# Norm roots as powers on GpSimd, silu as tanh, in a streaming-encoder layer on one core

## The reference, cut to what matters

```python
def rms_scale(x):
    return x * lax.rsqrt(jnp.mean(x * x, axis=-1, keepdims=True) + 1e-6)

h = rmsnorm(x, g_mix)                       # norm 1
q, k, v, g, gb, gc, hc = split(h @ w_in)    # 4 x 512 and 3 x 512 columns
o = rms_scale(retention(rotary(q), rotary(k), v))   # norm 2, for each of 4 heads
o = o * jax.nn.silu(g)
c = gb * short_conv(gc * hc)
x = x + concat([o, c]) @ w_out
h = rmsnorm(x, g_ffn)                       # norm 3
# peer(h), for each row: 8 heads x 16 chosen experts of 16384
act = gelu(dot(h, u_tab[eidx]));  x = x + sum(gate * act * v_tab[eidx])
y = rmsnorm(x, g_final)                     # norm 4
```

## Time and profile before

| | |
|---|---|
| median of 3 runs | 3035.3 us (3033.67 to 3039.89) |
| the profiled execution, its own time | 3035.47 us |
| span from its first to its last instruction | 3033.6 us |
| TensorE, VectorE, ScalarE, GpSimd busy | 76%, 68%, 67%, 40% of the span |
| moved by DMA | 1226.64 MB, mean 404 GB/s; the gathers 1107.36 MB of it |
| mean granted TensorE clock | 0.846 |

### The profile page before, as it was taken

How to read it: one execution, slowest core, us unless ns; L and a number is a source line. 1 busy time by engine, 2 the same in 40 slices (tenths; PEclk the granted TensorE clock), 3 DMA queues, 4 the chain that set the end, 5 groups by cost and what they waited for, 6 DMA issues and landing times.

```text
span 3033.6 us, 36636 instructions
## 1 busy us (share of the span) xinstructions
PE 2303.3 (76%) x12800; PEld 1880.0 (62%) x12800; DVE 2067.1 (68%) x5112; ACT 2044.8 (67%) x3704; POOL 1228.0 (40%) x1060
## 2 busy tenths in 40 slices
PE   9976887787668887877777877888777766667666
PEld 7765776665557766656566665665556555555555
DVE  2466887566688775666888744566588899955454
ACT  1277666668677566776677666667767777676666
POOL 0133333334333333444443344433344445456653
PEclk9987989998889889987887998989888886666666
DMA  7599999999999999999999999999999999999998
GB/s 301 190 416 397 413 408 414 419 420 413 420 421 409 420 417 415 420 404 420 420 416 406 404 422 419 419 419 396 405 420 420 418 418 409 415 418 419 422 420 333
DMA packets 180568, 1226.64 MB, mean 404 GB/s; under 512 B 20736, under 2 KB 21952, under 8 KB 40736
## 3 DMA queue, kind: packets, MB, share of 16 engines
q0 software_dynamic: 152064, 1107.36, 88.6%
q1 hardware_dynamic: 28032, 116.88, 9.6%
q10 hardware_dynamic: 288, 0.07, 0.0%
HBM read 1219.37 MB, written 4.86 MB: 404 GB/s over the span
## 4 chain that ended last, share of the span: by engine, by line
DMA 35%; DVE 24%; PE 22%; ACT 13%; issue 5%; POOL 1%; DVEq 0%; POOLq 0%; ACTq 0%
DMA ring<-in_uv,idx 35%; DVE ring L1459 12%; PE expert_sum L1116 8%; ACT ring L873 5%; PE mm L914 4%; PE x_ps L976 3%; ACT weights L869 2%; PE mm L1038 2%; PE mm L923 2%; ACT L860 1%; DVE pairs_left L1306 1%; ACT dots L860 1%; DVE pairs_left L1394 1%; DVE top_i L1315 1%; DVE pick_f L1400 1%
## 5 line engine op out<-in xcount | busy, mean ns | idle before, releaser
L661 POOL DMA_INDIRECT ring<-in_uv,idx x1056 | 1227.7, 1163 | 1781.8 <-PE expert_sum L1116 1574.7
L1116 PE MATMUL expert_sum<-ident_sb,ring 128*128 128x128 f32 x8448 | 1367.1, 317 | 581.3 <-ACT ring L873 579.8
L1459 DVE CUSTOM_DVE_ANT_0 ring<-ring,xn 128x1024 f32<-128x1024 f32 x1056 | 1286.7, 1223 | 737.8 <-DMA ring<-in_uv,idx 730.2
L1116 PEld LDWEIGHTS expert_sum<-ident_sb,ring 128*128 128x128 f32 x8448 | 1150.5, 165 | 838.6 <-ACT ring L873 767.9
L873 ACT ACTIVATE ring<-ring,weights 128x1024 f32<-128x1024 f32 x1056 | 1213.2, 1149 | 34.3
L860 ACT ACTIVATE dots<-dots 128x1 f32<-128x1 f32 x1056 | 211.5, 200 | 771.6 <-DVE dots L1459 768.2
L869 ACT ACTIVATE weights<-dots,gate 128x1 f32<-128x1 f32 x1056 | 311.1, 295 | 38.2
L914 PE MATMUL mm<-stream,xn_in 128*128 128x256 f32 (+1 forms) x912 | 258.4, 421 | 71.9 <-ACT qkvg L708 56.3
L1038 PE MATMUL mm<-turn,stream 128*128 128x256 f32 (+2 forms) x1024 | 278.4, 401 | 2.8 <-DVE xn_in L1155 2.8
L914 PEld LDWEIGHTS mm<-stream,xn_in 128*128 128x128 f32 (+1 forms) x912 | 166.9, 199 | 113.7 <-ACT qkvg L708 66.0
L923 PE MATMUL mm<-xn_in,stream 128*128 128x256 f32 (+1 forms) x640 | 183.7, 426 | 34.8 <-ACT conv_tmp L699 22.6
(11 more groups left out here) (233 smaller groups left out, 1517.4 us busy)
## 6 DMA issues: line engine op xcount, KB each, us to landing
stream<-in_wq SPq DMA_DIRECT2D x36, 1024.0 KB, 12.0
stream<-in_w_ret SPq DMA_DIRECT2D x26, 1024.0 KB, 9.4
stream<-in_w_conv SPq DMA_DIRECT2D x24, 1024.0 KB, 11.9
ring<-in_uv,idx POOLq DMA_INDIRECT x1056, 12.3
ring<-in_w_ret SPq DMA_DIRECT2D x7, 1024.0 KB, 12.4
x<-in_x SPq DMA_DIRECT2D x8, 512.0 KB, 8.7
w_out_sb<-in_w_out SPq DMA_DIRECT2D x1, 4096.0 KB, 28.9
out_y<-xn SPq DMA_DIRECT2D x8, 512.0 KB, 11.9
```

The lines of the kernel that those rows point to most:

```text
L661: pool.indirect_dma_start(ring[:, g % RING, :], None, uv, bass.IndirectOffsetOnAxis(ap=rows, axis=0)).then_inc(landed[g % RING], 16)
L1116: ins = pe.matmul(expert_sum[:, c * P:(c + 1) * P], ring[:, g % RING, D + c * P:D + (c + 1) * P], ident_sb[:, :], is_transpose=True, start ...
L1459: dve.tensor_tensor_reduce(u, u, xn[:, t % 3, :], 1.0, 0.0, ALU.mult, ALU.add, dots[:, g % RING:g % RING + 1]).then_inc(dotted, 1)
```

## The change

The `Sqrt` on ScalarE and the reciprocal on VectorE of every norm are gone. In their place GpSimd adds epsilon to the mean square and raises it to the power -0.5, with a tensor of -0.5 as the exponent (`root`, two instructions with a wait between them). The division by the row length moves into the squares: `scale=ROOT_D` on ScalarE, a factor 1/128 on VectorE. There are 36 norms (4 kinds on 9 tiles), so 36 `Sqrt` and 36 reciprocals go and 72 small GpSimd instructions come. GpSimd's pieces stand between the gathers: what is due at slot s is written after gather s + 7 and before gather s + 8.

Silu(g) becomes (tanh(g/2) + 1) * g on VectorE, and its half goes into the product with the retention's output. Tanh is ScalarE's. It writes `qT`, so ScalarE waits for the scores read from it, and the query copies into `qT` wait for `silu_done`.

ScalarE's program had 140 table loads and has 58: 28 before `Exp`, 29 before gelu and one at the start. 43 loads before `Sqrt` or `Silu` are gone (the one at the start stands before the first square now), 39 before the gelu that followed them, and the first before `Exp`: 82 fewer in all. The squares of norm 1 are one slot earlier, the scaling of norm 3 two slots later (tile 0 apart).

```diff
+            pool.memset(minus_half[:, :], -0.5).then_inc(pool_op, 1)
+            done = [1]
+            def root(dst, mean, plus=EPS):
+                n, w = dst.shape[0], dst.shape[1]
+                pool.tensor_scalar(mean, mean, plus, None, ALU.add).then_inc(pool_op, 1)
+                done[0] += 1
+                pool.wait_ge(pool_op, done[0])
+                return pool.tensor_tensor(dst, mean, minus_half[0:n, 0:w], ALU.pow)
+            def root_of_x(t):
+                n, r = rows_of(t), RANK[t]
+                yield x_turn_at(t) - 3
+                pool.wait_ge(x_squared, r + 1)
+                root(stat[0:n, 9:10], stat[0:n, 8:9]).then_inc(x_root, 1)
...
             for g in range(TOTAL):
+                if g > RING:
+                    advance(programs, g - RING - 1)
...
-            act.activation(stat[:, 8:9], eps_sb[:, :], ACT.Sqrt).then_inc(root_table, 1)
...
-                yield x_turn_at(t) - 3
+                yield x_turn_at(t) - 4
...
-                act.activation(vg_of(t)[0:n, :], x_of(t)[0:n, :], ACT.Square,
+                act.activation(vg_of(t)[0:n, :], x_of(t)[0:n, :], ACT.Square, scale=ROOT_D,
                                accum_out=stat[0:n, 8:9]).then_inc(x_squared, 1)
-                act.wait_ge(x_squared, 2 * r + 1)
-                act.activation(stat[0:n, 8:9], stat[0:n, 8:9], ACT.Sqrt, bias=eps_sb[0:n, :],
-                               scale=1.0 / D).then_inc(x_squared, 1)
...
-                act.activation(g, g, ACT.Silu).then_inc(silu_done, 1)
+                if scores_before(at):
+                    act.wait_ge(first_keyed, 2)
+                    wait(act, keyed, scores_before(at) - 1)
+                act.activation(qT[0:n, :], vg_of(t)[0:n, RET:], ACT.Tanh, scale=0.5).then_inc(tanh_done, 1)
...
-                yield at + 16
-                act.wait_ge(ret_squared, r + 1)
-                act.activation(stat[0:n, 0:H], stat[0:n, 0:H], ACT.Sqrt, bias=eps_sb[0:n, :],
-                               scale=1.0 / P).then_inc(ret_rooted, 1)
...
+                    act.wait_ge(silu_done, sum(mix_at(t) < copy_at(m) for t in RANK))
...
+                yield at + 4
+                dve.wait_ge(tanh_done, r + 1)
+                g = vg_of(t)[0:n, RET:]
+                dve.scalar_tensor_tensor(g, qT[0:n, :], 1.0, g, ALU.add, ALU.mult).then_inc(silu_done, 1)
...
-                dve.wait_ge(ret_rooted, r + 1)
-                op(dve.reciprocal(stat[0:n, 0:H], stat[0:n, 0:H]))
-                settle()
+                dve.wait_ge(ret_root, r + 1)
...
-                yield at + 11
-                dve.wait_ge(x1_squared, 2 * r + 2)
-                op(dve.reciprocal(stat[0:n, 5:6], stat[0:n, 4:5]))
-                settle()
+                yield at + 13
+                dve.wait_ge(x1_root, r + 1)
...
-                dve.wait_ge(sum_squared, 2 * t + 2)
-                dve.reciprocal(stat[0:n, 7:8], stat[0:n, 6:7]).then_inc(sum_stat, 1)
-                dve.wait_ge(sum_stat, t + 1)
+                dve.wait_ge(sum_root, t + 1)
```

More of the change, by code:

```diff
@@ L36 @@
 EPS = 1e-6
+ROOT_D = D ** -0.5
 LOWEST = -3.0e38
@@ L333, in layer_kernel @@
         eps_sb = sb("eps_sb", [P, 1])
+        minus_half = sb("minus_half", [P, H])
         g_mix_sb = sb("g_mix_sb", [P, KC])
@@ L646, in _, with root_of_retention, root_of_x1, root_of_sum @@
         def _(pool):
+            pool.memset(minus_half[:, :], -0.5).then_inc(pool_op, 1)
[11 more added lines that the diff above has]
+                root(stat[0:n, 9:10], stat[0:n, 8:9]).then_inc(x_root, 1)
+            def root_of_retention(t):
+                n, r = rows_of(t), RANK[t]
+                yield mix_at(t) + 14
+                pool.wait_ge(ret_squared, r + 1)
+                root(stat[0:n, 0:H], stat[0:n, 0:H]).then_inc(ret_root, 1)
+            def root_of_x1(t):
+                n, r = rows_of(t), RANK[t]
+                yield out_at(t) + 10
+                pool.wait_ge(x1_squared, r + 1)
+                if r == 0:
+                    pool.wait_ge(first_squared, 2)
+                root(stat[0:n, 5:6], stat[0:n, 4:5], stat[:, 7:8] if r == 0 else EPS).then_inc(x1_root, 1)
+            def root_of_sum(t):
+                n = rows_of(t)
+                yield end_of(t) + 3
+                pool.wait_ge(sum_squared, t + 1)
+                root(stat[0:n, 7:8], stat[0:n, 6:7]).then_inc(sum_root, 1)
+            programs = started(*[root_of_sum(t) for t in range(TILES + 1)],
+                               *[stage(t) for t in RANK for stage in (root_of_x, root_of_retention, root_of_x1)])
+            for slot in range(FIRST, 0):
+                advance(programs, slot)
             for g in range(TOTAL):
+                if g > RING:
+                    advance(programs, g - RING - 1)
                 t, k = tile_of(g)
@@ L662, in _ @@
                                         bass.IndirectOffsetOnAxis(ap=rows, axis=0)).then_inc(landed[g % RING], 16)
+            for slot in range(TOTAL - RING - 1, LAST + 1):
+                advance(programs, slot)
         @block.scalar
@@ L738, in out @@
                     act.wait_ge(x1_half, 1)
-                    act.activation(xn_of(t)[:, 0:half], x1_of(t)[:, 0:half], ACT.Square,
+                    act.activation(xn_of(t)[:, 0:half], x1_of(t)[:, 0:half], ACT.Square, scale=ROOT_D,
                                    accum_out=stat[:, 6:7]).then_inc(first_squared, 1)
+                    act.wait_ge(eps_set, 1)
                     act.wait_ge(first_squared, 1)
-                    act.activation(stat[:, 7:8], stat[:, 6:7], ACT.Identity, bias=eps_sb[:, :],
-                                   scale=1.0 / D).then_inc(first_squared, 1)
+                    act.activation(stat[:, 7:8], stat[:, 6:7], ACT.Identity, bias=eps_sb[:, :]).then_inc(first_squared, 1)
                     act.wait_ge(x1_ready, 1)
-                    act.activation(xn_of(t)[:, half:], x1_of(t)[:, half:], ACT.Square,
+                    act.activation(xn_of(t)[:, half:], x1_of(t)[:, half:], ACT.Square, scale=ROOT_D,
                                    accum_out=stat[:, 4:5]).then_inc(x1_squared, 1)
[L747 to L750, removed]
                     return
@@ L1141, in norm @@
                 yield x_turn_at(t) - 1
-                dve.wait_ge(x_squared, 2 * r + 2)
-                op(dve.reciprocal(stat[0:n, 9:10], stat[0:n, 8:9]))
-                settle()
+                dve.wait_ge(x_root, r + 1)
                 for i in range(2):
@@ L1281, in out @@
                     yield at + 11
-                    dve.wait_ge(x1_squared, 2)
-                    op(dve.reciprocal(stat[:, 5:6], stat[:, 4:5]))
-                    settle()
+                    dve.wait_ge(x1_root, 1)
                     dve.wait_ge(g_ffn_in, 16)
```

50 lines of the change are left out of this document (14 added, 36 removed).

## The result

| | before | changed |
|---|---|---|
| median of 22 runs each | 3036.91 us | 3041.61 us |
| lowest to highest | 3031.6 to 3041.01 | 3038.4 to 3045.22 |
| ratio to before, 95% interval | | 1.0016 [1.001, 1.0023] |
| profiled run, its own time (span) | 3035.47 (3033.6) | 3045.22 (3043.4) |

The changed kernel is 4.7 us slower. The forecast was 2.5 us faster, and the measurement tells the two apart. The time lies inside the range of the forecast. All runs of the table are in the chip's usual state; one later run (3109.5 us, of e5) was slow and is not in its ratio. The profiled run is the highest of its 22, so I read places from this profile and amounts from medians.

The account below looks back on a forecast made before the run. The 16 DMA engines were taken to bound the loop. Terms of -3.5 (dips), 0, 0, +0.5 (tile 0's second norm) and +0.5 (last norm) made -2.5, so 3035.5 became 3033.0 us, range 3028 to 3042.

Parts of the forecast that it names:

- The roots in the loop: GpSimd's roots between gathers: fit its idle 1.6 us a gather, or the queue covers them; cost 0, bounds 0 and +3.
- signs of a wrong forecast: New dips behind GpSimd roots, first transposes later than 9.2 us, VectorE's scalings waiting for GpSimd over a step.
- Last norm: End of the program: root to scaling took 0.51 us, with a root of 1.0 costs +0.5, bounds -0.2 and +2.0.
- The dips: Loop windows with DMA share below 0.985: 700, 910, 1310, 2150 near removed loads; gain -3.5 us, bounds 0 and -9.5.
- All that faster engines can give back: In the loop, nine windows below full DMA share lack 9.5 us, taken as the cap on any gain there.
- The reload of the library: Before the first root: GpSimd's code reload, held at 0; as rival, 12.3 us gives 3041.7; chance of ending slower 13%.
- Tile 0's retention: Before the loop: 1.97 us of cover for a root of 1.0, cost 0; with a root of 2.5, +0.5.
- Tile 0's second norm: Before the loop: root and reciprocal took 0.53 us; with a root of 1.0 costs +0.5, bounds -0.2 and +2.0.
- The move of norm 3's scaling: In the loop, two slots later: VectorE only loses a lead of which the queue takes no notice; no cost.
- table loads are time: Rival, whole kernel: 105 us of loads and 11 of roots come off the end, 2920 us; chance 1%.
- the power is slow: Rival, all roots: 5 us or more each holds gathers and single chains, 3046 us or more; chance 6%.
- More dips go: Rival, loop: all 9.5 us back gives 3026.0 to 3027; chance of more than 6.1 us gained 11%.

Follow-up runs that it names:

- e5: Changed kernel with only norm 1's root two gathers earlier in GpSimd's queue: 3034.53 us, ratio 0.999 to before.
- e7: Kernel before plus 36 unread pairs of root instructions on GpSimd at the changed kernel's places, no engine waiting for them: 3036.67 us, ratio 0.9998.
- e9: e7 with VectorE's norm 1 made to wait for GpSimd's unread root, all tiles but the first two: 3044.86 us, ratio 1.0025 to before.
- e1: Changed kernel with norm 1's root two gathers earlier and the last norm's one earlier on GpSimd: 3034.03 us, ratio 0.9988 to before.
- e3: Kernel before with only silu changed to tanh on ScalarE and a product on VectorE: 3035.47 us, ratio 0.9997.
- e8: Changed kernel with VectorE's scaling of norm 3 back at its old slot, its root left in place: 3048.3 us, ratio 1.0037 to before.
- e2: Kernel before with VectorE also waiting for TensorE's step ahead of norm 1's and the last norm's reciprocal: 3039.36 us, ratio 1.0009.

## Why the prediction was wrong

Two steps failed, each by about as much as the whole loss of 4.7 us or more, and a third, off the other way, hid part of it.

**The first step that failed** is "The roots in the loop", which the sum held at 0 with bounds 0 and +3. Its first half held: a root fits into GpSimd's idle time (e7, nothing measurable for 48 us of added work). Its second half saw VectorE's new wait and dismissed it: "where VectorE runs ahead it loses a lead of which the queue takes no notice". The queue does take notice. The wait at norm 1 is worth +7.1 us taken out of the changed kernel (e5) and +8.2 us put into the kernel before (e9), more than twice the upper bound. Two things were missed. "Met with little to spare" was reckoned with the mean step of 2.5 us, but a wait falls where TensorE is furthest behind its mean, after a piece of its own: GpSimd sat 7.81 us at that gather, and already sat there 6.90 us in before. And VectorE's lead is what refills ScalarE and TensorE during the catch-up; with it gone, TensorE stands again, and the gathers are issued up to 4 us later, and the five in flight did not cover that. It was also listed among the signs of a wrong forecast (scalings that wait for GpSimd for more than a step, new dips behind roots), without a price of its own among the rivals.

**The second step that failed** is "Last norm", which the sum held at +0.5 with bounds -0.2 and +2.0. It priced the way from the root to the scaling (+0.39, below) and let "the write of y" follow it. What it lacked is the end of GpSimd: with the root as its last work, its DRAIN lasts past SyncE's, and the end is 4.15 us longer in all seven profiles of kernels with that root at the end, and in none of the five others. The term is +4.5.

**What the sum makes of this.** With norm 1's wait gone (e5), the time is 2.3 us below before, ratio 0.999 [0.998, 0.9999], where the sum said -2.5. That this fits is luck: e5 still pays 4.5 at the last norm and 0.45 at tile 0's second. Taken off, they leave some -7.3 for all the rest (an estimate; with the interval of e5's ratio, -5 to -11) where the sum held the dips at -3.5. The last dots of e5's profile agree in sign, 5.4 us earlier than in that of before. The changed kernel has these terms and the wait at norm 1 on top. The terms of the sum, one by one:

- The dips (-3.5, bounds 0 and -9.5): three of the four went (700, 1310, 2150); 910 stayed, at 0.91. That isn't the new wait's doing, as it is 0.92 in e1 and 0.86 in e3. The two table loads and the root between steps are gone from the place of the earlier trace rows. 260, which I had put down to a pair for `Exp`, went as well (in e1 it is 0.91); its cause was not tried. The sum of the dips also misses what the loop gained: e5's windows lack 11.1 us, more than the 9.5 of before, and yet its dots end 5.4 earlier. "All that faster engines can give back" was not shown by that sum, and what gave the rest back is open.
- The reload of the library (0, the slower rival): the reload itself takes 7 to 11 ns in the profile at 0.8 us, the first root's two instructions start at 5.79 and 6.10 for 0.23 and 0.57 us, and the first projections at 10.87, against 10.75 in before. e7 has the same reload with nothing to hide behind: it is at 0.80 and the first add starts at 0.96, with its usual 0.23 us. The rival falls.
- Tile 0's retention (0): the scaling starts at 64.86, against 64.74 for the reciprocal in the earlier trace rows, 0.56 us after the root is done. Hidden.
- Tile 0's second norm (+0.5) and the last norm (+0.5). The earlier trace rows had 0.53 and 0.51 us from the root's start to the scaling; the changed kernel (timeline):

```profile
103.87 0.30 POOL L654 TENSOR_SCALAR stat<-stat 128x1 f32<-128x1 f32 x1 [39.57 <-ACT xn L781]
104.25 0.57 POOL L657 TENSOR_TENSOR stat<-stat,minus_half 128x1 f32<-128x1 f32 x1
104.85 1.42 DVE L1303 SCALAR_TENSOR_TENSOR xn<-x,stat,g_ffn_sb 128x512 f32<-128x512 f32 x2 [1.84 <-POOL stat L657]
...
3034.61 0.22 POOL L654 TENSOR_SCALAR stat<-stat 32x1 f32<-32x1 f32 x1 [20.55 <-ACT xn L864]
...
3035.51 1.27 DVE L1452 SCALAR_TENSOR_TENSOR xn<-x_ps,stat,g_fin_sb 32x1024 f32<-32x1024 f32 x1 [3.55 <-POOL stat L657]
```

  That is 0.98 and 0.90: +0.45 and +0.39. Behind the last scaling come the 4.15 us of the second failed step.
- Silu (nothing): held, within what the runs can tell (e3).
- The move of norm 3's scaling, "of the same kind" and so at 0: right in the changed kernel, but for another reason than the one given. It keeps VectorE off a wait that costs 6.7 us (e8).
- The rival "table loads are time" (2920) fell with the result, and "the power is slow" with 0.57 us for the power of one column. "More dips go" didn't come either: e1, without the waits at norm 1, still lacks 9.9 us in its windows, though its last dots, too, are 5.4 us earlier than in before.

**What stays open:** the places of the rest of e9's loss; why e2's wait of 3.04 us costs less than its share; the dip near 1630; where the loop gained more than its dips; and what GpSimd's DRAIN does for 8.3 us. To leave the sample tile's last root on ScalarE and VectorE should give the 4.15 us back, as an estimate from the ends of e7 and e9; it was not tried. Of the kernels that were run, e1 is the better version of this change: ratio 0.9988 [0.9979, 0.9997], a little faster than before and clearly faster than the changed kernel.

## What to carry to other kernels

Price a wait by its place in the queue of the engine that will answer it: what stands ahead of it there, who releases that, and how late that one is at its worst, not on average. The lead of an engine that runs ahead of a full queue is needed when the others catch up, so it isn't free to spend. A helper's instruction that it needs belongs so early in the helper's order that it is done when asked for (here two gathers earlier gave 7 us back). To size such a wait, add it alone to the kernel before, with the real answering instruction in its real place; a stand-in that ends sooner undersizes it. And look at the end of the program: an engine that gets the last piece of work may be slower to finish than the one that had it, and a forecast that is right in sum can hide two terms that are wrong.

## What the runs showed of the hardware

A power of -0.5 on GpSimd took 0.57 us for one column of 128 rows and 1.05 for four. It grew where a dot of VectorE was under way (timeline of the changed kernel):

```profile
1978.64 1.23 DVE L1470 CUSTOM_DVE_ANT_0 ring<-ring,xn 128x1024 f32<-128x1024 f32 x1 [1.10 <-DMA ring<-in_uv,idx]
1978.67 2.10 POOL L657 TENSOR_TENSOR stat<-stat,minus_half 32x4 f32<-32x4 f32 x1
```

2.10 us is 1.05 more than the usual, about what was left of the dot; an add that took 0.23 elsewhere took 1.18 in the same position, at 691.05. VectorE's dot kept its 1.23, as it did where the power had begun first (power at 630.01 for 1.05, dot at 630.49). The Trainium skill (SBUF — State Buffer, section "Who interferes with whom") says that a VectorE instruction with two inputs in SBUF contends with a GpSimd instruction that reads SBUF, and that the one issued later waits. The trace agrees where GpSimd is the later one, with those numbers; where VectorE is the later one it shows no longer dot. None of this was on the path by itself (e7).

GpSimd's DRAIN at the end took 8.27 to 8.29 us in the seven profiles where a power was its last work and all gathers had landed long before, against 1.40 for TensorE's, 1.13 for ScalarE's and 1.31 for VectorE's in the changed kernel. Where a root was done 22 us ahead of the end (e7) its DRAIN took 13.8 us and delayed nothing. The reload of GpSimd's library took less than 0.2 us until the first add (e7).
